# Filling attention in small pieces with three value banks, and moving small loads and input steps of an encoder layer on eight cores

## What is computed

```python
u = rmsnorm(h, norm1_g);  proj = u @ w_in               # (B, 2048, 2560): q 1024 | k 256 | v 256 | f 1024
q = axial_rope(rmsnorm(q, q_norm_g)); k = axial_rope(rmsnorm(k, k_norm_g))
a_out = rmsnorm(attention_group(q, k, v), attn_out_g)   # 8 query heads, 2 kv heads, bidirectional softmax
f_out = rmsnorm(fourier_group(f, w_fmix), fourier_out_g)# Re(2-D DFT over positions and 128 channels), group map
h = h + concat([a_out, f_out]) @ w_out
up = depthwise_conv3(rmsnorm(h, norm2_g) @ w_up)        # 2 * 5632 channels
h = h + (silu(gate) * val) @ w_down
return rmsnorm(h, final_g)
```

## Time and profile before

| what | value |
|---|---|
| median of 3 runs | 1536.48 us (1533.08 to 1684.23) |
| the profiled execution | 1536.72 us, slowest core 6 |
| its span, first to last instruction, on core 6 | 1535.2 us (the eight cores: 1522.0 to 1535.2) |
| TensorE busy | 1456.6 us (95% of the span) |
| VectorE, ScalarE, GpSimd busy | 708.7, 455.3, 68.9 us |
| matmuls and transposes | 10115 |
| mean granted TensorE clock of core 6 | 0.986 of full |

### The profile page before, as it was taken

One profiled execution on the slowest core, in us unless ns is written; L12 is line 12 of the kernel. 1 busy time (PEld: TensorE's weight loads), 2 busy tenths in 40 slices (PEclk: granted clock), 3 DMA queues, 4 the chain that ended last, 5 costly groups with the idle time before them and its releaser, 6 DMA issues.

```text
span 1535.2 us, 25333 instructions; the slowest of 8 cores (1522.0 to 1535.2 us)
## 1 busy us (share of the span) xinstructions
PE 1456.6 (95%) x10115; PEld 884.9 (58%) x10115; DVE 708.7 (46%) x979; ACT 455.3 (30%) x795; POOL 68.9 (4%) x97
## 2 busy tenths in 40 slices
PE   5789899899879999999999999999999999999997
PEld 2334444566659666666654566664456665446655
DVE  2166467644455556444442244443234444223477
ACT  3266451377763222222210022220012222002244
POOL 1112120000000000000000000000000000000000
PEclk9999999999999999999999999999999999999999
DMA  9886314301406706353234543524454524255306
GB/s 215 162 191 175 75 29 92 56 1 42 97 1 181 124 1 110 55 101 65 52 73 80 93 90 55 97 42 76 78 94 72 94 42 77 56 102 103 63 1 220
DMA packets 44117, 131.74 MB, mean 86 GB/s; under 512 B 3809, under 2 KB 13026, under 8 KB 43874
## 3 DMA queue, kind: packets, MB, share of 16 engines
q0 software_dynamic: 23856, 90.44, 33.6%
q1 hardware_dynamic: 19858, 38.63, 7.9%
q10 hardware_dynamic: 288, 1.05, 0.4%
HBM read 212.16 MB, written 8.39 MB: 144 GB/s over the span
## 4 chain that ended last, share of the span: by engine, by line
PE 87%; DMA 4%; DVE 4%; issue 2%; ACT 2%; SPq 0%; DVEq 0%; ACTq 0%; POOL 0%; POOLq 0%
PE psum L213 87%; DMA arena<-xT_own 2%; DVE arena L235 2%; ACT arena L229 2%; DMA arena<-xT_oth 1%; DVE arena L241 1%; DMA arena<-rope 1%; PE psum L217 1%; DVE arena L907 0%; DVE arena L239 0%; DVE arena L257 0%; SPq L260 0%; DVE arena L252 0%; DVEq L1420 0%; DVEq L173 0%
## 5 line engine op out<-in xcount | busy, mean ns | idle before, releaser
L213 PE MATMUL psum<-arena 128*128 128x344 bf16 (+8 forms) x9881 | 1447.6, 307 | 65.7 <-ACT arena L229 19.6
L213 PEld LDWEIGHTS psum<-arena 128*128 128x128 bf16 x9881 | 869.7, 98 | 625.9 <-issue 89.8
L241 DVE SCALAR_TENSOR_TENSOR arena<-psum,arena 128x1026 f32<-128x1026 f32 (+1 forms) x208 | 248.8, 1204 | 351.7 <-ACT arena L229 331.8
L229 ACT ACTIVATE arena<-psum,arena 128x1026 f32<-128x1026 f32 (+6 forms) x127 | 130.0, 1026 | 756.9 <-PE psum L213 756.2
L235 DVE TENSOR_TENSOR arena<-psum,arena 128x512 f32<-128x512 f32 (+8 forms) x250 | 163.2, 657 | 280.0 <-PE psum L213 216.1
L229 ACT ACTIVATE arena<-arena 128x4 f32<-128x4 f32 (+12 forms) x284 | 156.7, 566 | 202.8 <-DVE arena L235 135.6
L229 ACT ACTIVATE arena<-psum 128x1024 bf16<-128x1024 f32 (+5 forms) x271 | 170.6, 665 | 110.2 <-PE psum L213 73.7
L235 DVE TENSOR_TENSOR arena<-arena 128x256 f32<-128x256 f32 (+8 forms) x265 | 170.7, 673 | 44.7 <-ACT arena L229 18.0
L245 DVE TENSOR_SCALAR arena<-arena 128x1024 bf16<-128x1024 f32 (+5 forms) x49 | 33.7, 714 | 66.3 <-DMA arena<-xT_own 37.9
L241 DVE SCALAR_TENSOR_TENSOR arena<-arena 128x342 bf16<-128x342 f32 (+4 forms) x100 | 55.9, 601 | 4.4 <-ACT arena L229 2.7
L260 POOL DMA_DIRECT2D arena<-wup x22 | 16.4, 745 | 558.2 <-PE psum L213 520.2
(11 more groups left out here) (22 smaller groups left out, 16.6 us busy)
## 6 DMA issues: line engine op xcount, KB each, us to landing
arena<-wup POOLq DMA_DIRECT2D x22, 2048.0 KB, 15.2
arena<-wdn POOLq DMA_DIRECT2D x12, 1536.0 KB, 11.5
arena<-xT_nat SPq DMA_DIRECT2D x16, 513.0 KB, 12.9
arena<-win POOLq DMA_DIRECT2D x4, 2048.0 KB, 25.2
arena<-xT_oth SPq DMA_DIRECT2D x16, 512.0 KB, 4.8
arena<-wout POOLq DMA_DIRECT2D x4, 2048.0 KB, 22.0
arena<-xT_own SPq DMA_DIRECT2D x14, 513.0 KB, 11.0
arena<-rope SPq DMA_DIRECT2D x34, 128.0 KB, 3.4
```

The source lines that it names most:

```text
L213: return S_.op("pe", lambda e: e.matmul(out, lhsT, rhs, start=start, stop=stop, skip_group_check=skip), reads, writes)
L229: return S_.op("act", lambda e: e.activation(out, in_, func, **kw), reads, writes)
L241: return dve(lambda e: e.scalar_tensor_tensor(out, in0, scalar, in1, op0, op1), reads, writes)
```

## The change

- P1: the three small loads and `rope_fill(4)` move behind chunk 15 (k == 15): first `gk_bc`, then the four rope tiles, then `ident` and `gq_bc`.
- P2: the group of own key/value tiles has four tiles instead of five; tiles 4 to 7 are single `kv_tile` calls, beginning with bank 6.
- P2: `oth_step` runs twice in query tiles 4, 6 and 8; the remaining sums of squares and `x_r1(False)` move behind the first query tile of the next loop.
- The `ab_unit` steps leave the filling and run behind each of the last four `fold_pair` calls, in bank 7, evicted on ScalarE.
- The filling: each unit is cut into parts (two matmuls of a z unit, four transposes, four matmul pairs of an output tile, pieces of the halo units); one part is taken in every pair, two in pairs 0 and 1. z units use bank 7 alone, in the order of groups 4 to 7, 0 to 3; group 4 is evicted on ScalarE. From pair 75 the filling rotates banks 6 and 7.
- The value accumulators of heads 0 to 8 of the 16 (query block, head) pairs rotate banks 4, 5 and 6; the others use 4 and 5. Each bank is divided by itself, and in a head's first pair the matmuls of the first bank come first. Squares and sums are put two pairs later.
- The early output tiles are filling parts: two halves of 512 columns, each copied by itself; the final scaling is put two pairs later. `attn_fin`, the h loads and `wx` move to pair 70.
- At pair 128 `out_mm(OT[4])` stands behind `pv_pair(126)` instead of before it.

```diff
-            if k == 7:
+            if k == 15:
+                dma("sp", gk_bc, gk_d.partition_broadcast(128), [], [("gk_bc", 0)], "c_gk")
+                rope_fill(4)
                 dma("sp", ident, ident_d, [], [("ident", 0)], "c_ident")
                 dma("sp", gq_bc, gq_d.partition_broadcast(128), [], [("gq_bc", 0)], "c_gq")
-                dma("sp", gk_bc, gk_d.partition_broadcast(128), [], [("gk_bc", 0)], "c_gk")
             if k in paced:
                 load_win_pieces(3, [2], "wk", [[("uO", k)]], i=s3, p0=3 + (k + 1) // 2, k0=5 + k)
-            if k == 13:
-                rope_fill(4)
...
-            for t in range(5):
+            for t in range(4):
                 mm(ps(2 + t), uO[:, k, t * 128:(t + 1) * 128], w2[:, k, :], k == 0, k == 15,
                    [("uO", k), ("wv", k), ("slot", s2)], [("ps", 2 + t)])
         s4 = load_win(4)
         for t in range(4):
             kv_post(t, 2 + t)
-        psacc_ctr[0] = 0
-        bank = proj(own_lhs(5 * 128), 128, uOk, s2)
-        flush(2)
-        kv_post(4, 6)
-        kv_post(5, bank)
-        for t in range(6, 8):
+        psacc_ctr[0] = 4
+        for t in range(4, 8):
...
+            if t in (4, 6, 8):
+                oth_step()
...
-        while done[1] < 16:
-            x_stat(False, done[1], None)
-            done[1] += 1
-        x_r1(False)
...
+            if t == 0:
+                while done[1] < 16:
+                    x_stat(False, done[1], None)
+                    done[1] += 1
+                x_r1(False)
...
+        def ab_unit(i):
+            for g in (2 * i, 2 * i + 1):
+                for a in range(2):
+                    c = (2 * (g % 2) + a) * 128
+                    mm(ps(7)[:, c:c + 128], ccs[:, a, :], wfb[:, g * 128:(g + 1) * 128], True, True,
+                       [("ccs", 0), ("wfb", 0)], [("ps", 7)])
+            pv = ps(7).rearrange("p (g a d) -> p g a d", g=2, a=2)
+            ks = [("AB", 2 * i), ("AB", 2 * i + 1)]
+            act(AB[:, 2 * i:2 * i + 2, 0:2, :], pv, AF.Copy, [("ps", 7)], ks)
+            act(AB[:, 2 * i:2 * i + 2, 2, :], pv[:, :, 1, :], AF.Copy, [("ps", 7)], [("ABm", i)], scale=-1.0)
...
+            ab_unit(t)
...
+        zbanks = [7]
 
         def z_bank():
-            b = 6 + zb[0] % 2
+            b = zbanks[zb[0] % len(zbanks)]
...
         def z_unit(g, par, a):
-            def go():
-                b = z_bank()
+            st = {}
+
+            def part(ts):
+                if 0 in ts:
+                    st["b"] = z_bank()
+                b = st["b"]
                 rank = par == 0 and a == 0
-                for t in range(4):
+                for t in ts:
                     ap, key = fold_at(par, a, t, g)
                     mm(ps(b, NF), ap, csf[:, 2 * par + a, t, :], t == 0, t == 3 and not rank,
                        [key, ("CSF", 0)], [("ps", b)])
+                if 3 not in ts:
+                    return
                 if rank:
                     mm(ps(b, NF), f_lo[0:1, 4, g * 128:(g + 1) * 128], rkt[0:1, :], False, True,
                        [("f_lo", 4, g // 4), ("rkt", 0)], [("ps", b)])
-                copy_any(1, ZT[:, a, g, par:2 * NF:2], ps(b, NF), [("ps", b)], [("ZT", a, g, par)])
-            return go
+                copy_any(0 if g == 4 else 1, ZT[:, a, g, par:2 * NF:2], ps(b, NF), [("ps", b)], [("ZT", a, g, par)])
+            return [lambda: part((0, 1)), lambda: part((2, 3))]
...
-        fill = collections.deque([ab_unit(i) for i in range(4)])
-        for g in range(8):
+        fill = collections.deque()
+        for g in (4, 5, 6, 7, 0, 1, 2, 3):
             for a in range(2):
                 for par in range(2):
-                    fill.append(z_unit(g, par, a))
-        fill.extend([halo_s, halo_pv, halo_tr, halo_f, halo_ss])
+                    fill.extend(z_unit(g, par, a))
+        nop = lambda: None
+        halo = [halo_s(), halo_pv(), [halo_tr] + halo_f(), [halo_ss, nop, nop, nop]]
+        later = collections.defaultdict(list)
+        B3 = (4, 5, 6)
...
+            n = p // 8
+            bk = (B3[2 * n % 3], B3[(2 * n + 1) % 3]) if n < 9 else (4, 5)
+            order = [(j, tl) for j in range(2) for tl in range(4)]
+            if sp == 0:
+                order = [(j, tl) for u in range(2) for j in range(2) for tl in (2 * u, 2 * u + 1)]
+            for j, tl in order:
                 sc = 2 * sp + j
-                for tl in range(4):
-                    c = (tl % 2) * 129
-                    mm(ps(4 + tl // 2)[:, c:c + 129], PT[p % NP][:, j * 512 + tl * 128:j * 512 + (tl + 1) * 128],
-                       Vaug[:, sc, h // 4, 0:129], sc == 0 and tl % 2 == 0, sc == 15,
-                       [("PT", p % NP), ("V", sc), ("V", 99)], [("ps", 4 + tl // 2)], skip=True)
+                c = (tl % 2) * 129
+                mm(ps(bk[tl // 2])[:, c:c + 129], PT[p % NP][:, j * 512 + tl * 128:j * 512 + (tl + 1) * 128],
+                   Vaug[:, sc, h // 4, 0:129], sc == 0 and tl % 2 == 0, sc == 15,
+                   [("PT", p % NP), ("V", sc), ("V", 99)], [("ps", bk[tl // 2])], skip=True)
             if sp < 7:
                 return
             rl, rlk = stat_slot(4)
             rlkeys = stat_keys(rlk)
-            pv = psum_t[:, 4 * 512:6 * 512].rearrange("p (b c) -> p b c", c=512)[:, :, 0:258].rearrange(
-                "p b (t c) -> p b t c", c=129)
-            pk = [("ps", 4), ("ps", 5)]
-            rl4 = rl.rearrange("p (b t) -> p b t", t=2).unsqueeze(3)
-            recip(rl4, pv[:, :, :, 128:129], pk, rlkeys)
-            tt(O_sb[:, :, h, :].rearrange("p (b t) c -> p b t c", t=2), pv[:, :, :, 0:128],
-               rl4.to_broadcast([128, 2, 2, 128]), ALU.mult, pk + rlkeys, [("O_sb", h)])
-            stt(sqa.rearrange("p (t c) -> p t c", t=4), O_sb[:, :, h, :], 1.0 / 1024.0, O_sb[:, :, h, :], ALU.mult,
-                ALU.mult, [("O_sb", h)], [("sqa", 0)])
-            red(ssh[:, :, h], sqa.rearrange("p (t c) -> p t c", t=4), [("sqa", 0)], [("ssh", h)])
+            for b in range(2):
+                pv = ps(bk[b], 258).rearrange("p (t c) -> p t c", c=129)
+                recip(rl[:, 2 * b:2 * b + 2].unsqueeze(2), pv[:, :, 128:129], [("ps", bk[b])], rlkeys[2 * b:2 * b + 2])
+                tt(O_sb[:, 2 * b:2 * b + 2, h, :], pv[:, :, 0:128],
+                   rl[:, 2 * b:2 * b + 2].unsqueeze(2).to_broadcast([128, 2, 128]), ALU.mult,
+                   [("ps", bk[b])] + rlkeys[2 * b:2 * b + 2], [("O_sb", b, h)])
+
+            def squares():
+                stt(sqa.rearrange("p (t c) -> p t c", t=4), O_sb[:, :, h, :], 1.0 / 1024.0, O_sb[:, :, h, :], ALU.mult,
+                    ALU.mult, [("O_sb", 0, h), ("O_sb", 1, h)], [("sqa", 0)])
+                red(ssh[:, :, h], sqa.rearrange("p (t c) -> p t c", t=4), [("sqa", 0)], [("ssh", h)])
+            if n < 15:
+                later[p + LAG + 2].append(squares)
+            else:
+                squares()
...
+        def out_early(t, it):
+            i0, st = (128 * (t - 4), 1) if t >= 4 else (1 + 128 * (3 - t), 2)
+            sb = {}
+
+            def part(j):
+                if j % 2 == 0:
+                    sb["b"] = z_bank()
+                b = sb["b"]
+                for g in (2 * j, 2 * j + 1):
+                    for a in range(2):
+                        mm(ps(b)[:, (g % 4) * 128:(g % 4 + 1) * 128], ZT[:, a, g, i0:i0 + 128],
+                           AB[:, g, a * st, :], a == 0, a == 1,
+                           [("ZT", a, g, 0), ("ZT", a, g, 1), ("AB", g), ("ABm", g // 2)], [("ps", b)])
+                if j % 2 == 1:
+                    c0 = 256 * (j - 1)
+                    dve(lambda e: e.tensor_copy(fcp[:, c0:c0 + 512], ps(b)), [("ps", b)], [("fcp", j // 2)])
+                if j < 3:
+                    return
+                ms, sk = stat_slot(1)
+                mskeys = stat_keys(sk)
+                fk = [("fcp", 0), ("fcp", 1)]
+                stt(sqj, fcp, 1.0 / 1024.0, fcp, ALU.mult, ALU.mult, fk, [("sqj", 0)] + mskeys, accum=ms)
+                r, rkeys = rstd_from_ms(ms, mskeys, 128, 1)
+                later[it[0] + 2].append(lambda: tsc(f_n[0], fcp, r[:, 0:1], None, ALU.mult, None, fk + rkeys,
+                                                    [("f_n", 0)]))
+            return [lambda j=j: part(j) for j in range(4)]
...
-            if p == 99:
+            if p == 70:
                 assert not fill
                 f_n = [A.alloc("f_n", o_wf, 2048, BF16)]
-                fcp = A.alloc("fcp", R_F + 6 * 4104, 4096, F32)
-                sqj = A.alloc("sqj", R_F + 6 * 4104 + 4096, 2048, BF16)
                 A.alloc("hA", R_F, 6 * 4104, F32)
                 load_h(range(6))
                 wx = A.alloc("wx", R_A, 16384, BF16)
                 dma("pool", wx, wout_d[:, 8192:16384], [], [("wx", 0)], "c_wx", max_dma_last_dim=8192)
-            if p in ET:
-                out_mm(OT[ET.index(p)])
-                out_norm(OT[ET.index(p)])
-            if p - 4 in ET:
```

(24 more changed lines are left out.)

148 lines of the change are left out of this document (71 added, 77 removed).

## The result

The changed kernel takes 1508.26 us (median of 4 runs). Its ratio to the kernel before is 0.9826, 95% interval 0.9803 to 0.985: 26.7 us less, between 23 and 30. The profiled execution took 1507.3 us with a span of 1505.7 us on its slowest core, 4. A second series of the same kernel gave 0.9816 (0.9799 to 0.9834). The forecast was 1507 us, and within 2% of the kernel before had its highest chance, 0.56; its terms came out less evenly than the total.

A forecast was written before the change was run, and what follows sets the result against it. TensorE, busy 1456.6 of 1535.2 us, was taken as the bound, so only its gaps and lowered clock could yield time. Terms -3.5 -3.9 +0.5 -7.0 -2.5 -3.5 -9.6 = -29.5 on 1536.7 gave 1507 us, range 1496 to 1523.

The forecast's parts named there:

- so the queue is empty sooner: Key tiles: weight loads start about 5 us earlier, helping remove all 3.6 us of waits for rope.
- I expect half of that back: Second half of attention: of some 6 us lost to the lower clock, half returns, -3 us.
- Input phase, -3.5: Before the key tiles: loads moved behind the last x^T chunk shorten TensorE's wait for chunk 12; bounds 0 and -6.3 us.
- Four key tiles, -3.9: First key/value tiles: bank wait replaced by a later 1.8 us one, gain 0.3, and 3.6 us of rope waits gone.
- Two chunks, +0.5: Query tiles: three extra conversions and squares cost +0.5 us, between 0 and +2.25, with VectorE already busy 32.35 of 36.
- -7.0 behind it: After the query tiles: 5.4 us wait for squares and 1.6 us of lower clock go, nothing else late; bounds -5 and -7.2.
- Attention, -15.6 on core 6: Attention in three terms: entry -2.5, first half -3.5, second half -9.6 us.
- The logarithm's four: Second half of attention: four TensorE waits behind a Fourier tile's logarithm on ScalarE shrink from 2.2 to 1.2 us each.
- rival A: After 285 us the clock never falls with gaps of at most 1.2 us: 1500 us; chance 0.27.
- rival B: Front gives nothing, late rope holds blocks, VectorE bounds query tiles, logarithm's wait stays 2 us: 1519 us; chance 0.25.
- Rival C: Attention: bank 7's turn-around stops TensorE at each z unit and the clock drops: 1547 us; chance 0.05.
- The rule of the Trainium skill: Cycling through PSUM banks with micro-idles makes the clock swing, so one-bank z units would lose clock; time given in rival C.

The follow-up runs named there:

- b_loads: Kernel before with only the small loads and four rope tiles moved behind chunk 15; P1 52.5 us against 57.6, key tiles 48.5 against 48.3.
- six later executions: Later executions of kernels with the same front edits as the changed kernel, itself included; key tiles 46.0 to 46.7 us, query tiles 35.3 to 35.7.
- b_key4: Kernel before with only four own key tiles in the group instead of five; key tiles 46.2 us against 48.3.
- b_oth: Kernel before with only two chunks at a time and the later sums; query tiles 35.25 us against 34.65, stretch behind them 87.25 against 95.1.
- a_two: Changed kernel with value banks 4 and 5 for all heads, each still divided by itself; from second query loop through attention 223.5 us against 218.75.
- a_ab: Changed kernel with AB units back at the head of the filling, evicted on VectorE; from second query loop through attention 227.65 us against 218.75.
- a_whole: Changed kernel with each early output tile's four parts in one pair, then three empty ones; second query loop through attention 224.1 us against 218.75.
- a_same: The changed kernel itself run once more for comparison; ratio to the kernel before 0.9816, median 1508.3 us.

## Why the prediction was right, and where it was not

The total was right (-29.5 forecast; -26.7 by the ratio, -29.5 by the spans of the slowest cores), and partly by luck, because terms of opposite sign were off. On core 6, from whose rows the terms were worked out, the stages gave -4.4, -3.1, +2.0, -7.0 and -17.4, together -30.0.

Two steps of the prediction failed. The mechanism that failed is that of the key tiles, "so the queue is empty sooner": it was to take rope waits away, and b_loads, which has it alone, has as many as before. The term that was furthest off is the clock in attention, "I expect half of that back": forecast -4.4 with the entry's share, and TensorE's busy time in the stretch fell by 7.9 us on core 6. It was hidden in the total by gaps that shrank by 9.5 us instead of 10.8 and by the query tiles. Term by term:

- **Input phase, -3.5:** -4.3, by b_loads about -5. That fits the bytes' arithmetic (3.8 us) and about 1 us of clock; but the clock stays up before the last chunks on five cores of eight only. The products in front of block 0 hide, as said: no core waits for it.
- **Four key tiles, -3.9:** -2.7, and -1.6 to -2.3 in the six later executions. The new wait at tile 1 was forecast at 1.8 us and is 1.9. The failed step is "the queue is empty sooner": b_loads took nothing from this stage. What removes most rope waits is the other half of the sentence, buffers released earlier (b_key4, -2.1), and up to 1 us for rope stays on single cores.
- **Two chunks, +0.5:** +1.7, and +0.6 to +1.1 in the six later executions. The step forgot that sums move with the conversions: 24 columns of statistics, 0.6 us (b_oth). The rest is a stall behind ScalarE on some cores, in b_oth too; VectorE, which I took for the risk, was not it.
- **-7.0 behind it:** -6.7, by b_oth -7.8 alone. The wait and the clock went whole; "nothing else is late" was wrong, block 1 is, by 0.5 to 2.4 us on six cores.
- **Attention, -15.6 on core 6:** -17.4 there, -14.8 on the median core. At the entry the waits are 2.3 us, as forecast. In the first half the head changes were undersized: 0.45 us a head by my row, 4.8 us over nine heads in a_two. A head of eight pairs, 9.84 us before (first two rows, core 6), takes 9.30 after (last two rows, core 4), as the divisions of two heads in succession show. In a_two it is 9.90 again (core 3), so dividing each bank by itself gained nothing there, and the third bank gained all of it:

```profile
312.02 0.18 DVE L252 RECIPROCAL arena<-psum 128x4 f32<-128x4 f32 x1
...
321.86 0.18 DVE L252 RECIPROCAL arena<-psum 128x4 f32<-128x4 f32 x1
...
297.77 0.17 DVE L252 RECIPROCAL arena<-psum 128x2 f32<-128x2 f32 x1
...
307.07 0.17 DVE L252 RECIPROCAL arena<-psum 128x2 f32<-128x2 f32 x1
```

  In the second half the waits are 9.1 us, forecast 8.0. The logarithm's four were forecast at 4.8 us and are three, 3.3 us. Not foreseen: 1.5 us at the halo sum, whose VectorE product stands behind an output tile's product sum, 0.35 us behind the logarithm of `attn_fin`, and 0.4 us instead of 0.3 at each later head change.
- **The clock,** "expect half back": all of it came back in attention. From q2 TensorE is busy 214.6 us before and 206.75 after on core 6 for the same matmuls, 7.9 us less against 4.4 forecast, so 3.5 more. This was rival A's mechanism, with waits up to 1.5 us where it asked for 1.2; its 1500 us did not come because gaps, key tiles and query tiles together gave some 4 us less. None of rival B's parts came true; block 1's lateness is not among them.
- **Rival C** did not come: the z units on one bank have no wait for it from 290 to 360 us. a_ab shows how near it was: the one bank cost 6.9 us of waits and a clock at 0.83 over 20 us as soon as an eviction stood behind the fold's work on VectorE.

The rule of the Trainium skill weighed in the prediction ("TensorE: Matmul & The Clock Gate", section "A second HAM failure mode: psum-queue depth-cycling") is not borne out by the changed kernel. The filling cycles through one bank there, and from 290 to 360 us core 1 has 69.58 of 70 us of TensorE at clock 1.00, the others 68.7 or more. Among the runs that change the new kernel the clock fell again in attention only in a_ab and a_whole, with single waits of 2 us and more.

## What to carry to other kernels

A gap in the bounding engine costs itself and what its clock loses behind it; compare cores, since a stage that differs between them by microseconds and is the same in work is one whose clock falls. Cut filling so that no unit's eviction chain stands in front of the engine that feeds the main loop: put a small scalar step (here a logarithm) in the queue only when its input is surely there. When a step is moved, move its price with it, also the small matmuls that come with it.

## What was not expected of the hardware

In attention waits at or under 1.5 us, even seven and more in 70 us, left the granted clock at 1.00 on all eight cores, while in the kernel before four waits of 2.2 us stood beside some 6 us of clock loss over 90 us on core 6 (an estimate from the 0.92 of the earlier trace rows), and less on other cores.

But the length of a single wait does not decide it. In the kernel before, core 6 was at 0.79 of full from 392 to 400 us, though none of its waits from 304 to 394 us was over 0.7 us. A wait of 2.46 us at 53.35 left core 4 of the changed kernel at 1.00, and two of 2.0 and 2.7 us left cores 2 and 5 of a_whole there. In a_same, the same kernel as the changed one, the clock of cores 0, 5 and 6 is 0.89 from 70 to 85 us, where the only waits are the 0.5 and 1.4 us at the first two tails; the same two waits left all cores at 1.00 in the changed kernel's profile. That is why the key tiles' stage is 45.6 us in one execution and 46.7 in the other. What else decides stays open.

And loads that land earlier need not shorten the stage that waits for them: in b_loads four of five rope loads land sooner, and the key tiles' stage is 48.5 us against 48.3.
